# Decay differences of a chunked state-space scan: from broadcast running-sum products clipped on ScalarE to split-row products clipped on VectorE, on one Trainium2 core

## What is computed

```python
# 24 heads of 64 in 4 groups of 6, state 128, chunks of 128 tokens; 8 chunks
acs_l = jnp.cumsum(dtc * a.reshape(G, R), axis=2)          # running sums within a chunk
seg = acs[..., :, None] - acs[..., None, :]
decay = jnp.exp(jnp.where(tril, seg, -jnp.inf))
cb = jnp.einsum('bclgn,bcsgn->bcgls', cc, bc)
att = cb[:, :, :, None] * decay
y_diag = jnp.einsum('bcgrls,bcsgrp->bclgrp', att, xdt)
states = jnp.einsum('bclgn,bclgrp->bcgrpn', bc, xdt * decay_to_end[..., None])
h = h * chunk_decay + states                               # from chunk to chunk
y_off = jnp.einsum('bclgn,bcgrpn->bclgrp', cc, h_start) * jnp.exp(acs_l)
y = y_diag + y_off + d_skip * x                            # then * silu(z), grouped RMSNorm
```

## Time and profile before

| what | value |
|---|---|
| median of 3 runs | 2557.5 us (2556.35 to 2563.99) |
| time of the profiled execution | 2559.11 us |
| its span | 2557.4 us |
| PE busy | 2151.4 us, 84% |
| DVE busy | 972.7 us, 38% |
| ACT busy | 842.9 us, 33% |
| POOL busy | 381.9 us, 15% |
| mean granted clock of TensorE | 0.918 |
| `stage_ssd`, first transfer issued to first transfer of the next stage | 791.67 to 1018.25 us |

### The profile page before, as it was taken

The page is one execution under the profiler, slowest core; times in us unless marked ns, Lnnn a source line. Parts: engine busy times, 40 slices in busy tenths (PEclk is TensorE's granted clock), DMA queues, the critical chain, the costliest instruction groups (busy, mean ns, idle before and its releaser), DMA issues. The chain is left out here.

```text
span 2557.4 us, 32546 instructions
## 1 busy us (share of the span) xinstructions
PE 2151.4 (84%) x11725; PEld 1864.1 (73%) x11726; DVE 972.7 (38%) x1139; ACT 842.9 (33%) x1302; POOL 381.9 (15%) x511
## 2 busy tenths in 40 slices
PE   2999899999986886759978787866879759999992
PEld 2778799999985665539977687345767748887881
DVE  2214255520115774462114130033331354586572
ACT  4331123222213775240002231022111134686572
POOL 0000000000003996310110000010000101122112
PEclk9999899999997998879999899999989569999996
DMA  4111233322212221532334020301610627799885
GB/s 151 68 42 49 63 93 96 89 72 86 96 63 64 87 86 56 136 99 84 125 110 167 1 58 25 131 33 39 224 66 10 251 91 255 230 378 312 294 270 186
DMA packets 224834, 309.19 MB, mean 121 GB/s; under 512 B 12338, under 2 KB 144594, under 8 KB 224722
## 3 DMA queue, kind: packets, MB, share of 16 engines
q1 hardware_dynamic: 189716, 252.65, 29.1%
q0 software_dynamic: 6912, 25.17, 4.0%
q10 hardware_dynamic: 28144, 30.54, 3.5%
HBM read 242.19 MB, written 66.14 MB: 121 GB/s over the span
## 5 line engine op out<-in xcount | busy, mean ns | idle before, releaser
L308 PE MATMUL psum<-hT_high,t_w_high 128*128 128x352 f32 x960 | 311.0, 324 | 9.8 <-DVE t_w_low L727 9.8
L309 PE MATMUL psum<-hT_low,t_w_high 128*128 128x352 f32 x960 | 310.8, 324 | 0.0
L310 PE MATMUL psum<-hT_high,t_w_low 128*128 128x352 f32 x960 | 310.7, 324 | 0.0
L2689 ACT ACTIVATE e_w_high<-big 128x2048 fp32r<-128x2048 f32 x96 | 178.7, 1908 | 34.0 <-PEq L2175 26.3
L308 PEld LDWEIGHTS psum<-hT_high,t_w_high 128*128 128x128 f32 x960 | 181.3, 189 | 10.3 <-issue 10.3
L309 PEld LDWEIGHTS psum<-hT_low,t_w_high 128*128 128x128 f32 x960 | 181.3, 189 | 0.0
L310 PEld LDWEIGHTS psum<-hT_high,t_w_low 128*128 128x128 f32 x960 | 181.3, 189 | 0.0
L2773 DVE TENSOR_TENSOR e_w_low<-big,e_w_high 128x2048 fp32r<-128x2048 f32 x64 | 144.0, 2289 | 39.2 <-ACT e_w_high L2689 38.3
L2632 PE MATMUL psum<-e_w_high,e_xT_high 128*128 128x512 f32 x368 | 148.5, 404 | 6.4 <-DVE e_xT_low L2768 4.3
L2633 PE MATMUL psum<-e_w_low,e_xT_high 128*128 128x512 f32 x368 | 146.4, 398 | 0.0
L2634 PE MATMUL psum<-e_w_high,e_xT_low 128*128 128x512 f32 x368 | 146.3, 398 | 0.0
(11 more groups left out here) (419 smaller groups left out, 4478.4 us busy)
## 6 DMA issues: line engine op xcount, KB each, us to landing
big<-in_w_expert_gate SPq DMA_DIRECT2D x32, 1024.0 KB
big<-in_w_expert_up SPq DMA_DIRECT2D x32, 1024.0 KB, 8.1
big<-in_w_expert_down SPq DMA_DIRECT2D x32, 1024.0 KB
t_w<-in_w_in SPq DMA_DIRECT2D x24, 512.0 KB, 4.3
x_scr<-t_conv_out ACTq DMA_DIRECT2D x20, 512.0 KB, 4.3
gate_scr<-t_conv_in ACTq DMA_DIRECT2D x16, 528.0 KB, 2.7
m_gates<-gate_scr SPq DMA_DIRECT2D x16, 528.0 KB, 5.3
big<-in_x_prompt SPq DMA_DIRECT2D x2, 4096.0 KB, 17.9
```

Source lines behind the costliest of these rows:

```text
L308: nc.tensor.matmul(out, ah, w_h, start=start, stop=False)
L309: nc.tensor.matmul(out, ah, w_l, start=False, stop=False)
L310: return nc.tensor.matmul(out, al, w_h, start=False, stop=stop)
L2689: return nc.scalar.activation(dst, src, ACT.Copy)
```

## The change

The difference of two running sums becomes a product with a contraction over 14 rows. `stage_rows` turns the running sums (eight transposes after block j = 2), splits them into a high and a low F32R part, makes the negatives of both, and stores the four planes to `acs_scr`. In `stage_ssd` a tile `dec` of 14 rows takes the place of `s_dta`. Its first 768 columns are the moving operand: rows 0 and 1 are the high and low sums of the six heads, rows 2 to 13 are patterns of ones that pick a head. Its last 128 columns are the stationary operand: two rows of ones, then the negated high and low sums of the six heads. Patterns and ones are written by POOL once, at the stage's start; the sums come with three transfers a step from SP. Two F32R products of 384 columns give all six heads' differences. VectorE clips them in one operation from PSUM into `s_att`, and ACT does the Exp alone. The clip stands first in VectorE's step. SP's loads are written out by step, and at the start they wait for POOL's patterns. The gate tensors of the merge are computed and stored where they were.

The core of the diff (renamings of semaphores and of `last` to `last_`, allocations and counts are left out):

```diff
@@ stage_rows, sync
             sp.wait_ge(s_vo, NT)
             sp.dma_start(g.out["gv"], g.v[0:NS, NT - 1, :]).then_inc(g.s_out, g.stored())
+            sp.wait_ge(s_ahr, 2)
+            for i in range(2):
+                sp.dma_start(g.acs_scr[2 * i], ah[:, i, :].bitcast(F32)).then_inc(s_ast, 16)
+                sp.dma_start(g.acs_scr[2 * i + 1], al[:, i, :].bitcast(F32)).then_inc(s_ast, 16)
+            sp.wait_ge(s_ast, 64)
@@ stage_rows, tensor, after the tiles of block j
+                if j == 2:
+                    pe.wait_ge(s_dta, 5)
+                    for t in range(NC):
+                        tr = nc.tensor.transpose(ps[0:H, 6 + t // 4, (t % 4) * P:(t % 4 + 1) * P], g.acs[:, t, :],
+                                                 g.ident[:])
+                    tr.then_inc(s_at, 1)
@@ stage_rows, scalar, after block j = 2
+            def sums_high():
+                act.wait_ge(s_at, 1)
+                src = ps[0:H, 6:8, :].rearrange("p b t -> p (b t)")
+                nc.scalar.activation(ah[:, 0, :], src, ACT.Copy).then_inc(s_ahr, 1)
+                act.wait_ge(s_alr, 1)
+                nc.scalar.activation(ah[:, 1, :], ah[:, 0, :].bitcast(F32), ACT.Copy, scale=-1.0)
+                nc.scalar.activation(al[:, 1, :], al[:, 0, :].bitcast(F32), ACT.Copy, scale=-1.0).then_inc(s_ahr, 1)
@@ stage_rows, vector, after w_low(3)
+            dve.wait_ge(s_ahr, 1)
+            nc.vector.tensor_tensor(al[:, 0, :], ps[0:H, 6:8, :].rearrange("p b t -> p (b t)"),
+                                    ah[:, 0, :].bitcast(F32), ALU.subtract).then_inc(s_alr, 1)
@@ stage_ssd
+    DR = 2 + 2 * R
+    DW_ = R * P
-        dtc = g.sb("s_dta", [P, 2, H], ctx=ctx)
+        dec = g.sb("s_sums", [DR, 2, DW_ + P], F32R, ctx=ctx)
@@ sync
+            def load_sums(c, gg):
+                q, hs, ts = gg % 2, slice(R * gg, R * gg + R), bass.ds(c * P, P)
+                sp.dma_start(dec[0:2, q, 0:DW_].bitcast(F32).rearrange("s (r t) -> s r t", t=P), g.acs_scr[0:2, hs, ts]).then_inc(s_dl[q], 16)
+                for i in range(2):
+                    sp.dma_start(dec[2 + R * i:2 + R * i + R, q, DW_:DW_ + P].bitcast(F32), g.acs_scr[2 + i, hs, ts]).then_inc(s_dl[q], 16)
+            def body(c, first, last_):
+                for gg in range(G):
+                    n = c * 4 + gg
+                    sp.wait_ge(s_rb, n + 1)
+                    if gg < 2:
+                        load_sums(c, gg + 2)
+                    elif not last_:
+                        load_sums(c + 1, gg - 2)
+                    if not last_:
+                        sp.wait_ge(s_yo, n + 1)
+                        load(c + 1, gg)
+                    def next_z(cc, g2):
+                        sp.wait_ge(s_yz, cc * 4 + g2 + 1)
+                        load_z(cc + 1, g2)
+                    if not (last_ and gg >= 2):
+                        before(c, gg, 2, first, next_z)
+            sp.wait_ge(s_dc, 1)
+            for gg in range(2):
+                load_sums(0, gg)
             for gg in range(G):
                 load(0, gg)
                 load_z(0, gg)
@@ tensor, front
-                pe.wait_ge(s_rl, n)
-                pe.wait_ge(s_dtc, c * 2 + gg // 2 + 1)
-                for r in range(R):
-                    a = dtc[:, gg // 2, gg * R + r:gg * R + r + 1].to_broadcast([P, P])
-                    mm = nc.tensor.matmul(ps[:, RB + r // 3, (r % 3) * P:(r % 3 + 1) * P], a, g.tri[:],
+                pe.wait_ge(s_dl[q], c * 96 + (gg // 2) * 48 + 48)
+                pe.wait_ge(s_mn, n)
+                for j in range(2):
+                    mm = nc.tensor.matmul(ps[:, RB + j, 0:XW], dec[:, q, DW_:DW_ + P], dec[:, q, j * XW:(j + 1) * XW],
                                           start=True, stop=True)
@@ scalar
-                act.wait_ge(s_rb, n + 1)
-                act.wait_ge(s_yd, n + 1)
-                for r in range(R):
-                    e = nc.scalar.activation(att[:, q, r, :], ps[:, RB + r // 3, (r % 3) * P:(r % 3 + 1) * P],
-                                             ACT.Relu, bias=g.acs[:, c, gg * R + r:gg * R + r + 1], scale=-1.0)
-                e.then_inc(s_rl, 1)
-                act.wait_ge(s_rl, n + 1)
-                nc.scalar.activation(att[:, q], att[:, q], ACT.Exp, scale=-1.0).then_inc(s_e, 1)
+            def exp(c, gg):
+                act.wait_ge(s_mn, n + 1)
+                nc.scalar.activation(att[:, q], att[:, q], ACT.Exp).then_inc(s_e, 1)
@@ vector
+            def clamp(c, gg):
+                dve.wait_ge(s_rb, n + 1)
+                dve.wait_ge(s_yd, n + 1)
+                nc.vector.tensor_scalar(att[:, q].rearrange("p (b r) t -> p b (r t)", b=2), ps[:, RB:RB + 2, 0:XW],
+                                        0.0, None, ALU.min).then_inc(s_mn, 1)
             def body(c, first, last_):
                 for gg in range(G):
+                    clamp(c, gg)
                     front(c, gg)
+                    rest(c, gg)
+                    before(c, gg, 1, first, back)
@@ gpsimd
-            def keep_dta(c, half):
-                nc.gpsimd.tensor_copy(dtc[:, half, :], g.dta[:, c, :]).then_inc(s_dtc, 1)
+            heads = [last(g.ident[0:DR, 2 + R * i:2 + R * i + R], P) for i in range(2)]
+            for q in range(2):
+                nc.gpsimd.tensor_tensor(dec[:, q, 0:DW_].rearrange("s (r t) -> s r t", t=P), heads[0], heads[1], ALU.add)
+                op = nc.gpsimd.tensor_copy(dec[:, q, DW_:DW_ + P], g.ones[0:DR, :])
+            op.then_inc(s_dc, 1)
```

More of the change, by code:

```diff
@@ L335, in stage_rows @@
         tot = g.etot
+        ah, al = g.acs_parts
+        s_at, s_ahr, s_alr, s_ast = (g.sem("r_acs_" + n) for n in ("turned", "high", "low", "stored"))
         s_w = [g.sem(f"r_w_loaded{i}") for i in range(2)]
@@ L484, in _ @@
                     decays()
+                if j == 2:
+                    sums_high()
             for s in range(3):
@@ L888, in stage_ssd @@
         s_zin = [g.sem(f"s_z_loaded{i}") for i in range(G)]
+        s_dl = [g.sem(f"s_sums_loaded{i}") for i in range(2)]
         s_tx, s_yo, s_rb, s_yd, s_st, s_yt = (g.sem("s_" + x) for x in (
-            "x_turned", "cb_and_yoff", "running_sums", "ydiag", "new_state", "y_turned"))
+            "x_turned", "cb_and_yoff", "differences", "ydiag", "new_state", "y_turned"))
         s_xr, s_e, s_ss, s_yn, s_ye = (g.sem("s_" + x) for x in (
             "x_rows", "exp", "squares", "y_normed", "yT_written"))
[L893 to L897, removed]
+        s_dc, s_mn, s_cbm, s_att, s_y1, s_y2, s_h = (g.sem("s_" + x) for x in (
+            "sums_patterns", "differences_clamped", "cb_masked", "att", "y1", "y2", "h_updated"))
+        s_xdd, s_hd, s_y3, s_yz, s_ms, s_rs = (g.sem("s_" + x) for x in (
+            "xdd", "h_decayed", "y3", "yz", "mean", "rstd"))
         s_ht, s_ho = g.sem("s_h_turned"), g.sem("s_h_rows_ready")
@@ L933, in _ @@
                 load_z(0, gg)
[L934 to L940, removed]
+            chunks(sp, body)
             sp.wait_ge(s_ho, 1)
@@ L946, in _ @@
         def _(pe):
-            pe.wait_ge(s_dtc, 1)
+            pe.wait_ge(s_dc, 1)
             def front(c, gg):
@@ L992, in back, with body @@
                                  stop=True).then_inc(s_st, 1)
-            def body(c, first, last):
+            def body(c, first, last_):
                 for gg in range(G):
@@ L998, in body @@
                         front(c, gg + 1)
-                    elif not last:
+                    elif not last_:
                         front(c + 1, 0)
@@ L1009, in _ @@
             pe.wait_ge(s_ye, STEPS)
+            pe.wait_ge(s_mn, STEPS)
             for j in range(XF):
@@ L1054, in write @@
             def write(c, gg):
-                n = c * 4 + gg
+                n, q = c * 4 + gg, gg % 2
                 act.wait_ge(s_yt, n + 1)
@@ L1061, in write, with body @@
                 a.then_inc(s_ye, 1)
-            def body(c, first, last):
+            def body(c, first, last_):
                 for gg in range(G):
                     rows(c, gg)
+                    exp(c, gg)
                     before(c, gg, 3, first, scale)
@@ L1095, in front, with rest @@
                                         last(g.eacs[:, c, gg * R:(gg + 1) * R], HD), ALU.mult).then_inc(s_y1, 1)
+            def rest(c, gg):
+                n, q = c * 4 + gg, gg % 2
                 dve.wait_ge(s_xr, n + 1)
-                dve.wait_ge(s_yd, n + 1)
                 nc.vector.tensor_tensor(hd(xdt[:, q, :]), hd(xrb[:, q, 0:XW]),
@@ L1113, in back, with body @@
                 nc.vector.tensor_tensor(h[:, gg, :], h[:, gg, :], ps[:, ST, 0:XW], ALU.add).then_inc(s_h, 1)
-            def body(c, first, last):
+            def body(c, first, last_):
                 for gg in range(G):
+                    clamp(c, gg)
                     front(c, gg)
-                    if gg:
-                        back(c, gg - 1)
-                    elif not first:
-                        back(c - 1, G - 1)
```

(12 more changed lines are left out.)

4 lines of the change are left out of this document (added).

## The result

The change made the kernel slower by 0.43%: the median of seven runs is 2571.77 us (2567.76 to 2574.2), beside 2562.47 us (2556.35 to 2563.99) for seven runs of the kernel before; the ratio is 1.0043, with an interval of 1.0031 to 1.0056. The profiled execution took 2571.77 us, its span is 2570.0 us (before 2557.4 us), its mean granted clock 0.904 (before 0.918).

The account below looks back on a forecast made before the run. Two closed rings through POOL, with DVE and with ACT, were taken to bound the scan step. 6.6 - 2.4 + 0.6 - 1.2 - 0.6 + 1.1 = +4.1 on 2557.5 gave 2561.6 us; range 2552 to 2570, likeliest case 2556.5 to 2567.

Parts of the forecast that it names:

- the sum: Whole kernel: the terms for scan steps, scan start and rows stage added up to +4.1 us.
- six products to two: PE in each scan step: L968's 1.60 us become at most 0.81, taken as 0.5; gain 0.
- ring: Scan step: a closed chain of waits; one through DVE and POOL, 6.23 us, one through ACT and POOL, 6.20 us.
- four rivals: POOL freed (chances 0.09 and 0.07), clip blocking POOL (0.06), PE's low clock (0.10), dearer scan start (0.05).
- The steady step: Scan: the step stays 6.2 us, DVE's L1094 waits some 0.8 us for POOL, ACT's wait for POOL grows.
- The clip: VectorE in each scan step: 0.95 us, inside the 1.73 us wait for POOL; cost 0.
- rival 2: Scan steps: the clip blocks POOL, 0.95 us more a step, 2589 us; chance 0.06.
- rival 3: PE in the scan falls to the low clock: +68 us if it lasts, 2569 us if half the time; chance 0.10.
- the text's mark of 0.9: Scan's steady part: a PE clock below 0.9 with L985 late for y would show the forecast wrong.
- The scan's start: Patterns 3.5 us and six transfers 3.1 make first transposes 6.6 later; first steps change this by -2.4, +0.6 and -1.2.
- The rows stage: PE ahead of the scan: eight added transposes cost 1.1 us (0.5 to 2.2); other additions are covered.

Follow-up runs that it names:

- before_pad8: The kernel before plus 8 tiny unread products (32 instructions) on PE at the scan's start; 1.0023 of before, 2566.84 us.
- after_pad56: The changed kernel plus 56 tiny unread products on PE at the scan's start, making PE's list as long as before; 1.0014 of before, 2565.11 us.
- before_no_relu: The kernel before without differences, clip and Relus, the Exp reading the running sums from PSUM; wrong decays, 0.9842 of before, a step of 6.20 us.
- after_x_first: The changed kernel with x and z of two head groups loaded ahead of the wait for POOL's patterns; 1.0026 of before, 2568.27 us.
- the 60 products: 60 tiny unread products on PE at the scan's start, added to `rows_only`; 1.0024 of before, 2566.07 us.
- rows_only: The kernel before with only the change's `stage_rows` (transposes, split, four stores) and the old scan; 1.0011 of before, 2566.20 us.
- x_first_pad56: The changed kernel with x and z of two steps loaded ahead of the patterns' wait and 56 tiny products on PE; 1.0010 of before, 2563.29 us.
- act_xdd: `x_first_pad56` with L1138 (x times dte) moved from POOL to ACT as six scaled copies; 0.9891 of before, 2533.87 us.
- after: The changed kernel in its first group of runs, against the kernel before; 1.0043, 2571.77 us.
- after_again: The changed kernel, unedited, measured again in another group of runs against the kernel before; 1.0044, 2572.91 us.

## Why the prediction was wrong, and where it was right

**What failed is the end of the sum.** The working of "six products to two" ends with "No ring holds L968: gain 0", and the sum adds up the rows stage and the scan and takes everything behind `stage_ssd` as it was. The first is right for the scan. But the same edit makes PE's list 224 instructions shorter, and a shorter list moves each later code load. In this kernel one of them moved from behind the first K load into it: +1.2 us directly, and +6.9 us in all with what TensorE's clock then did. `before_pad8` shows this without any of the change, `after_pad56` takes some 7.7 of the 11 us back without undoing any of it. The rows stage and the whole of `stage_ssd` gave 0.7 and 0.6 us in the profiled pair, where the sum has 1.1 and 3.0; what lies behind `stage_ssd` gave 12.2 us, where the sum has nothing. None of the four rivals had its place behind the scan. The range failed with it, since it was made from bounds of the same terms. These bounds, added up again, give -0.3 to +7.2 us, 2557 to 2565 us, and not the 2556.5 to 2567 that stand there. The base was off too: it was the median of three runs, 2557.5 us, and that of seven is 2562.47. On that base the same sum gives 2566.6 us, and a range as wide around it would have held 2571.77 us; that would have been luck, since the missed step is the same.

**The steady step: right.** 6.20 us beside the predicted 6.2. The Relus held no ring (`before_no_relu`: 6.20). The clip took 0.94 us beside 0.95, DVE's wait for POOL is 0.86 us beside "some 0.8", ACT's wait for L1222 grew, and nothing waited for the running sums' transfers.

**The clip and POOL: right.** L1212 stayed at 994 to 1010 ns, under one clip and under two, so rival 2 is out. "VectorE: DVE Perf Modes" of the Trainium skill, which limits the two-port mode to SBUF operands, agrees. "SBUF — State Buffer" of the same skill lets `tensor_scalar` take the shared ports when its operands meet the conditions of that page, so read together they forecast no cost, as the prediction took it.

**The low clock of PE (rival 3): the mechanism came, its price did not.** The clock of the steady part fell to 0.85, below the text's mark of 0.9. But DVE waited for PE for only 3.6 us of 100, three times. PE's removed work paid for the lower level: it is busy for 85.14 us of 100, 87.06 before, and so its wait for y did not grow in the sum (14.2 us, 12.2 before) as the prediction had it. The Trainium skill ("TensorE: Matmul & The Clock Gate") warns of throttles that recur between bursts; here they recur and the step is no longer than before. Where such a fall did cost is the sample attention, where PE itself sets the pace.

**The scan's start: right in kind, too large.** The patterns took 3.4 us beside 3.5. The six transfers took 1.9 beside 3.1, as the small transfers started 0.32 us apart and not 0.52 as the x loads did, and x was there 2.9 us after its issue, where it had taken 3.75 (791.67 to 795.42). The transposes were 4.3 us late and not 6.6. With what the first steps gave back, the first product with `s_cb` was 1.3 us late, and the scan of this pair ended 0.5 us later and took 0.6 us more: the sum had +3.0 for it. `after_x_first` took back 3.9 us of the scan, so the start did cost about what was said of it. The old scan lies between 219.1 and 221.7 us in four profiles (224.1 with the 60 products), so that no single pair can settle a term of this size.

**The rows stage: right.** The eight transposes took 1.03 us, the stage became 0.7 us longer in the one pair and 1.7 in the other.

**Where the rest behind the scan lies.** In the sample scan and the product with `w_mem_o` it is again the granted clock: 0.80 over 107.4 us and 0.78 over 108.6 us, 0.92 over 116.8 us and 0.91 over 118.9 us. In the router it is not: its stretch has a mean clock of 0.50 before and 0.56 after, and is yet 2.1 us longer. There a wait of VectorE for a DMA transfer grew, here before and then after (total us, times, longest):

```profile
DVE o_xg L2360 <- DMA h_scr<-o_xg: 21.2, 3, 16.5
```

```profile
DVE o_xg L2411 <- DMA h_scr<-o_xg: 22.5, 2, 18.7
```

It goes with the place of a code packet as the wait for K does. Counted from the router's first transfer the packet moves at 33 to 34 us in the kernels before, in `rows_only` and in `after_pad56` (longest wait 16.3 to 16.6 us), at 15 to 16 us in the kernel after and `after_x_first` (18.6 to 18.7), and at 19 us in `before_pad8` (17.5).

**What stays open.** Why a K that is 1.2 us late costs so much of the clock. What moves the clock in the product and in the sample scan, whose 1.2 us came and went (107.5 in `after_pad56`, 108.7 in `x_first_pad56`). Of the 7 us in the sample attention 2.5 remain with K in time (a clock of 0.80 instead of 0.83), but not in `act_xdd`, where it took 79.1 us. And no run shows the packet moved without PE's list being changed.

## What to carry to other kernels

An edit that changes the number of instructions on an engine can move time in every later stage: compare the traces stage by stage before looking at the edited one, and where an untouched stage is longer, look for "instruction" packets beside its first loads. A few dummy instructions ahead of it tell that cause from one in the edited code, if they lie where the engine waits anyway: 60 products in the way of the scan's first transposes made them 2.5 us late. Freeing an engine that is in no closed ring gains nothing by itself; it is worth something when work of a ring is then moved onto it, here 1% from a change that alone cost 0.4%, and more so if that ends a blocking between two other engines.

## What the runs showed of the hardware

- Where a code packet of 0.02 MB fell 2.6 to 3.0 us behind the issue of a 1 MB load, the wait for it was 6.9 to 7.1 us instead of 5.5 to 5.8, in four profiles of three kernels (`after`, `after_again`, `after_x_first`, `before_pad8`).
- With a K 1.2 us late TensorE stayed at its lower level for 9.1 us behind the first product instead of 3.1, and the stage was 6.9 us longer; with the packet 8 us behind the issue, which delayed only the second load, it was 10.5 us longer (`rows_only`).
- Over 14 rows, a POOL operation of 768 columns took 1.45 us where 128 rows take 1.48: the columns count.
- DVE's two products of 384 columns took 0.90 and 1.18 us beside POOL's L1199 and L1204, and 0.59 and 0.55 us in `act_xdd`, where L1199 is gone and L1204 lies ahead of them.
